# A hybrid decoder layer on one core: the order of the first loads, and the last stage's squares and products over two PSUM banks at once

## The reference, cut to what matters

```python
def _rmsnorm(x, g):
    xf = x.astype(jnp.float32)
    y = xf * lax.rsqrt(jnp.mean(xf * xf, axis=-1, keepdims=True) + EPS)
    return (y * g.astype(jnp.float32)).astype(x.dtype)

def _layer(x, mem_k, mem_v, s5_re, s5_im, lru_h, lru_conv, w):
    h = _rmsnorm(x, w["g_mix"])
    proj = h @ w["w_in"]                 # the first projection
    ...                                  # S5 and RG-LRU heads, output projection, cross attention
    x = x + _hier_moe(x, ...)            # two experts for each token, weighted
    ...
y_prompt = _rmsnorm(xp, g_final)
y_sample = _rmsnorm(xs, g_final)
```

## Time and profile before

| | before |
|---|---|
| three executions, us | 1136.73, 1139.09, 1140.87 |
| median, us | 1139.09 |
| the profiled execution, us | 1138.03 |
| its span, first to last instruction, us | 1136.2 |
| mean granted TensorE clock | 0.991 |
| PE busy | 1092.9 us, 96% |
| PE weight loads busy | 617.8 us, 54% |
| DVE busy | 625.3 us, 55% |
| ACT busy | 250.6 us, 22% |
| POOL busy | 80.9 us, 7% |

### The profile page before, as it was taken

One profiled execution on the slowest core, in us unless ns is written; L12 is line 12 of the kernel. 1 busy time (PEld: TensorE's weight loads), 2 busy tenths in 40 slices (PEclk: granted clock), 3 DMA queues, 4 the chain that ended last, 5 costly groups with the idle time before them and its releaser, 6 DMA issues.

```text
span 1136.2 us, 15240 instructions
## 1 busy us (share of the span) xinstructions
PE 1092.9 (96%) x6149; PEld 617.8 (54%) x6149; DVE 625.3 (55%) x1250; ACT 250.6 (22%) x531; POOL 80.9 (7%) x108
## 2 busy tenths in 40 slices
PE   6999999999999999999999999999899999999985
PEld 4666766677765444788866645554433333333322
DVE  4676499927857655843277776775632121121256
ACT  5200321356641111100033311111301011111115
POOL 5000010101000000000000000000111112121110
PEclk9999999999999999999999999999899999999998
DMA  9109350277471002300055451016779999999968
GB/s 296 46 1 221 30 42 1 74 203 274 151 275 23 0 1 88 135 1 1 9 200 200 148 217 43 20 56 228 282 270 402 417 415 418 415 417 416 366 251 315
DMA packets 65368, 209.27 MB, mean 184 GB/s; under 512 B 13560, under 2 KB 22416, under 8 KB 57072
## 3 DMA queue, kind: packets, MB, share of 16 engines
q1 hardware_dynamic: 54528, 177.68, 43.9%
q0 software_dynamic: 10640, 30.55, 7.6%
q10 hardware_dynamic: 128, 0.03, 0.0%
HBM read 187.05 MB, written 28.53 MB: 190 GB/s over the span
## 4 chain that ended last, share of the span: by engine, by line
PE 90%; DVE 5%; issue 2%; DMA 1%; ACT 1%; ACTq 0%; SPq 0%; DVEq 0%; POOLq 0%
PE bank L713 15%; PE bank L1230 15%; PE bank L876 9%; PE bank L941 8%; PE bank L1247 7%; PE bank L1071 6%; PE bank L685 5%; PE bank L835 3%; PE bank L973 2%; PE bank L1038 2%; PE bank L1218 2%; PE bank L802 2%; PE bank L1115 1%; PE bank L983 1%; PE bank L858 1%
## 5 line engine op out<-in xcount | busy, mean ns | idle before, releaser
L713 PE MATMUL bank<-arena 128*128 128x360 f32 (+1 forms) x576 | 177.7, 468 | 1.0 <-DVE arena L1633 0.9
L1230 PE MATMUL bank<-arena 128*32 128x512 f32 x1536 | 171.7, 599 | 1.0 <-DVE arena L2349 1.0
L713 PEld LDWEIGHTS bank<-arena 128*128 128x128 f32 x576 | 108.5, 190 | 64.8 <-issue 1.5
L1230 PEld LDWEIGHTS bank<-arena 128*32 128x32 f32 x1536 | 47.7, 110 | 106.6 <-issue 105.3
L1952 DVE TENSOR_TENSOR arena<-arena,bank 128x512 f32<-128x512 f32 (+3 forms) x56 | 68.3, 1220 | 66.6 <-PE bank L941 37.5
L876 PE MATMUL bank<-arena 128*128 128x272 f32 x448 | 103.0, 392 | 0.0
L1071 PE MATMUL bank<-arena 128*128 128x512 f32 x224 | 100.6, 598 | 0.5 <-DVE arena L2117 0.5
L941 PE MATMUL bank<-arena 128*128 128x512 f32 x224 | 97.7, 593 | 0.0
L876 PEld LDWEIGHTS bank<-arena 128*128 128x128 f32 x448 | 85.0, 190 | 17.4
L2353 DVE TENSOR_TENSOR arena<-arena,bank 128x256 f32<-128x256 f32 x24 | 10.1, 420 | 150.7 <-ACT arena L1539 150.7
L1247 PE MATMUL bank<-arena 128*32 128x512 f32 x768 | 86.8, 592 | 0.6 <-ACT arena L1542 0.6
(11 more groups left out here) (424 smaller groups left out, 1336.1 us busy)
## 6 DMA issues: line engine op xcount, KB each, us to landing
arena<-in_w_gate SPq DMA_DIRECT2D x32, 1024.0 KB, 9.4
arena<-in_w_up SPq DMA_DIRECT2D x32, 1024.0 KB, 15.4
arena<-in_w_down SPq DMA_DIRECT2D x32, 1024.0 KB, 16.4
arena<-in_ck SPq DMA_DIRECT2D x8, 1024.0 KB, 7.2
arena<-in_cv SPq DMA_DIRECT2D x8, 1024.0 KB, 5.3
arena<-work_moe SPq DMA_DIRECT2D x16, 512.0 KB, 7.4
arena<-in_w_in SPq DMA_DIRECT2D x3, 2048.0 KB, 14.9
arena<-in_x SPq DMA_DIRECT2D x8, 512.0 KB, 6.0
```

What stands on the lines that cost most here:

```text
L713: last = nc.tensor.matmul(b[:, 0:w], win[slot][:, k, m * P:m * P + P], ht[:, k, c0:c0 + w], start=k == 0, stop=k == KD - 1)
L1230: last = nc.tensor.matmul(bank[2 + j % 2][t0:t0 + QT, :].rearrange("p (h n) -> p h n", h=2), xgt[j % 2][:, k, t0:t0 + QT], gu[e % GUB][:, ...
```

## The change

There are five edits.

1. SP's order at the front: tiles 0 to 2, then the first third of `w_in`, then the convolution state and nine vectors (`VECS[3:]`), then the three tables; then a wait for the `w_in` transfer to land, and then tiles 3, 4 and 5. Six of those vectors were on ACT's queue before.
2. ACT issues three vectors (`VECS[:3]`) rather than nine ahead of its table load.
3. The eight PSUM banks are one tensor, so that one instruction can read two neighbouring banks. ACT's work for a PE tile is then one square of 1024 columns and one root, rather than two squares, an identity and a root; DVE's is one product of 1024 columns rather than two of 512.
4. PE no longer waits for `fin_x` ahead of the identity products; inside the branch for overflowing experts it waits for one more semaphore (`xya_ok`) instead.
5. DVE's order at the end: sums of 8 and 0; output of 8; sum of 2; output of 0; sum of 4; outputs of 1 and 2; sum of 6; outputs of 3 to 7.

```diff
-        bank = [ctx.enter_context(nc.psum_tensor(f"bank{b}", [P, 512], f32)) for b in range(8)]
+        psum = ctx.enter_context(nc.psum_tensor("banks", [P, 8 * 512], f32))
+        bank = [psum[:, 512 * b:512 * b + 512] for b in range(8)]
...
             for n in range(3):
                 load_x(n)
+            load_win(0, 0)
             sp.dma_start(cstin[0:NB * 3 * CT, :], I["state_lru_conv"]).then_inc(sem["par_in"], 16)
-            for name, rows in VECS[9:]:
+            for name, rows in VECS[3:]:
                 sp.dma_start(parin[COL[name]:COL[name] + rows, :], I[name]).then_inc(sem["par_in"], 16)
-            load_win(0, 0)
-            load_x(3)
             for src, dst in ((I["lam_re"], q16[0:GP, 2, :]), (I["lam_im"], q16[0:GP, 3, :]), (I["log_dt"], ptmp[0:GP, 256:258])):
                 sp.dma_start(dst, src).then_inc(sem["lam_in"], 16)
-            for n in range(4, 6):
+            sp.wait_ge(sem["win_in0"], 16)
+            for n in range(3, 6):
                 load_x(n)
             load_win(1, DH)
...
+                pe.wait_ge(sem["xya_ok"], XT)
                 pe.wait_ge(sem["xyd_ok"], XT + len(ZORDER))
...
-            pe.wait_ge(sem["fin_x"], 1)
             pe.wait_ge(sem["f_dg"], 2 * len(FPE))
...
-            for name, rows in VECS[:9]:
+            for name, rows in VECS[:3]:
                 act.dma_start(parin[COL[name]:COL[name] + rows, :], I[name]).then_inc(sem["par_in"], 16)
...
-                    link(nc.scalar.activation(squaresf[:, 0:512], bank[2 * j][:, :], ACT.Square, accum_out=ssq[:, i:i + 1]))
-                    link(nc.scalar.activation(squaresf[:, 512:1024], bank[2 * j + 1][:, :], ACT.Square, accum_out=srs[:, j:j + 1]))
-                    link(nc.scalar.activation(srs[:, j:j + 1], srs[:, j:j + 1], ACT.Identity, scale=1.0 / D, bias=zero1[:, 1:2]))
-                    nc.scalar.activation(rstd[:, i:i + 1], ssq[:, i:i + 1], ACT.Sqrt, scale=1.0 / D, bias=srs[:, j:j + 1]).then_inc(sem["f_std"], 1)
+                    link(nc.scalar.activation(squaresf[:, :], psum[:, 1024 * j:1024 * j + 1024], ACT.Square, accum_out=ssq[:, i:i + 1]))
+                    nc.scalar.activation(rstd[:, i:i + 1], ssq[:, i:i + 1], ACT.Sqrt, scale=1.0 / D, bias=zero1[:, 1:2]).then_inc(sem["f_std"], 1)
...
-                    for hf in range(2):
-                        cols = slice(hf * 512, hf * 512 + 512)
-                        last = V.scalar_tensor_tensor(xres[:, i, cols], bank[2 * j + hf][:, :], rstd[:, i:i + 1], gfin[:, cols], MUL, MUL)
-                    last.then_inc(sem["f_out"], 1)
+                    V.scalar_tensor_tensor(xres[:, i, :], psum[:, 1024 * j:1024 * j + 1024], rstd[:, i:i + 1], gfin[:, :], MUL, MUL).then_inc(sem["f_out"], 1)
...
-            for i in (8, 0, 2):
+            for i in (8, 0):
                 fsum(i)
-            for i in (8, 0):
-                fout(i)
+            fout(8)
+            fsum(2)
+            fout(0)
             fsum(4)
-            for i in (1, 2):
-                fout(i)
+            fout(1)
+            fout(2)
             fsum(6)
```

## The result

The changed kernel takes 1141.36 us (median of 22 executions, 1139.6 to 1143.76), the kernel before, beside it, 1139.34 (22 executions, 1136.73 to 1142.2). The ratio is 1.0023 with a 95% interval of 1.0016 to 1.0029: slower by 2.6 us (1.8 to 3.3), inside 0.3%, where 1141.3 had been forecast. The two medians by themselves are 2.0 us apart. Beside e9, e10 and e11 the kernel before had two slow executions of 23, of 1177.63 and 2935.26 us, which the ratios leave out.

A forecast was written before the change was run, and what follows sets the result against it. PE's chain of waits (90% of the span) was taken as the bound, with DVE's work setting the end. Plus 4.0 at the front and minus 1.8 at the end gave 1139.09 + 2.2 = 1141.3 us, 8-in-10 range 1136.0 to 1144.0.

The forecast's parts named there:

- The small loads behind the weights: Front: ten small loads land after the weights on SP's queue, shifting the projection to 21.0 us, plus 4.0 us.
- The 14.1: Front: time in us when tiles 0 to 2, 13 small loads and first weights are all through, bounds 13.0 to 15.0.
- the 12%: Front: data rate lost in a us with small packets, some 0.3 us over the few, used for the lower bound.
- ACT's shorter list: Front: six fewer issues start tile 0's transposes 1.2 us earlier, worth nothing while PE waits for the vectors until 14.1.
- Tiles 3 to 5: Front: loads issued after the first weights land still come before PE asks, cover over 4 us, so nothing.
- DVE's order and the long products: Last stage: reordered DVE work and one product in place of two, together minus 1.8 us, bounds minus 0.8 to 2.4.
- The products' term: Last stage: one 1024-column product takes 1.28 us instead of a pair's 1.41, four times 0.13 saved, taken as 0.5.
- the term for DVE's order: Last stage: tile 8's output fills the hole ahead of tile 2's sum, which starts at 1116.64; minus 1.29 us.
- The cover of 5 us: End: DVE reaches tile 7 5 us after PE's last product ended, so PE's earlier identity products gain zero.
- B: Rival, front: small loads pass the weights, ACT's earlier start gives minus 1.2, total 1136.1 us; chance 0.16.
- C: Rival, front: PE idles, its clock rises only inside the projection, up to 3.3 us more, 1144.6; chance 0.16.
- D: Rival, last stage: two-bank reads or loads hold DVE, gaining only 0.3 us, total 1142.8; chance 0.08.

The follow-up runs named there:

- e9: Kernel before plus changed end, wide PE products, ACT's three-vector list, six other vectors on SP ahead of the first weights; 1133.71 against 1140.52 us, ratio 0.9943.
- e10: Kernel before with only tiles 3, 4 and 5 moved behind the wait for the first weights; 1139.5 against 1140.52 us, ratio 0.9994.
- e11: Kernel before plus only five 512-column identity products on PE at the front; 1138.82 against 1140.52 us, ratio 0.9982.
- e1: Changed front with the last stage of the kernel before; 1143.42 against 1138.74 us, ratio 1.0042.
- e3: Kernel before with only state_lru_h (16 KB) moved behind the first weights on SP's queue; 1143.9 against 1138.74 us, ratio 1.0041.
- e12: Changed kernel with the first weights issued behind the ten small loads, no products added; 1136.24 us against the kernel before's 1139.49, ratio 0.9978.
- e2: Front of the kernel before with the changed last stage; 1138.41 against 1138.74 us, ratio 0.9992.
- e5: Front of the kernel before, changed last stage, plus five 512-column identity products on PE at the front; 1136.0 against 1139.63 us, ratio 0.9975.
- e6: Changed kernel plus 512-column identity products: three ahead of tile 0, four in the wait, one after; 1139.25 us against the kernel before's 1139.63, ratio 1.0005.
- e7: Front of the kernel before, changed last stage, but PE's wait for fin_x put back; one execution, 1138.43 us.
- e8: Front of the kernel before, changed last stage, but DVE's old order (sums of 8, 0, 2 first); one execution, 1138.85 us.
- e4: Changed kernel plus 24 identity products of 128 columns on PE between tile 0 and the vectors' wait; 1138.91 us against the kernel before's 1138.74, ratio 1.001.

## Why the prediction was right

**The small loads behind the weights (plus 4.0).** Right in mechanism and near in size: 21.44 - 17.04 = 4.40 in the changed kernel and 4.02 in e1. The vectors' transpose, forecast at 14.1 and at most 15.0, came at 14.59 and 14.46. e3 shows the mechanism by itself, and e12 that the rest of the changed front costs nothing that its time can tell. The Trainium skill's ring order ("DMA: Bandwidth & Descriptors", section "Queues, rings and completion order") agrees with e3's 13.80. What the Trainium skill says in the section "Issuing engines are not separate DMA queues" of the same page, that issuing from several engines only saves issue time, does not fit e3: ACT's last small load was issued there at 3.99, behind the weights' 3.42, and ACT's queue was through by 9 us, while `state_lru_h`, issued at 3.88 on SP's queue, came at about 13.75. The reasoning that the same bytes are through at the same time in any order was off in its parts: the weights landed 1.3 us earlier than before, not a few tenths, and the small loads 1.8 us behind them. The sum of the two errors is half a us. The 14.1 was not the time of that set alone either: the DMA engines had moved 4.48 MB by then in the kernel before, and 3.79 in e10, where tile 3 was not behind the weights, which landed at 13.8 all the same. And the 12% were put down to small packets, but from 7 to 8 us the rate before was 329 GB/s with 36 of them among 192. The 6.92 us from the vectors' transpose to the projection were 6.85 and 6.60.

**ACT's shorter list (nothing here).** Right. PE was ready 1.3 us earlier and waited; the 1.3 us turn up as soon as the vectors are there (e12).

**Tiles 3 to 5 (nothing).** Right, by e10, whose interval runs from 1.7 us faster to 0.3 slower.

**DVE's order and the long products (minus 1.8).** Right in direction and mis-sized: minus 0.94 in the changed kernel and minus 1.21 in e2 by the trace; minus 0.9 us by time in e2, with an interval from minus 1.9 to plus 0.1. The products' term held: 1.28 us each, 0.13 saved. What was mis-sized is the term for DVE's order, in the start of tile 2's sum. It was put right behind tile 8's output, 1116.64 - 1112.45 = 4.2 us behind the first sum, with the load taken to come 4.1 us behind it, as in the one trace at hand; it came at 4.8 in both kernels, and DVE waited 0.5 us and took up 0.6 later than forecast. In the changed kernel another 0.2 us were lost to tile 1's root: PE, freed from its wait for `fin_x`, had finished its identity products early and then stood 4.34 us, and its next products ran at the lower level of the clock. (In e2 PE stood 4.40 us, the granted clock read 0.64 from 1114 to 1118 us, and nothing was lost at tile 1.) PE's timeline, and the stretch from 1122 to 1128 us, against the earlier trace rows:

```profile
1111.19 7.11 PE L1302 MATMUL banks<-arena,ident 128*128 128x512 f32 x16 [0.92 <-ACT arena L1546]
1122.64 10.05 PE L1306 MATMUL banks<-arena 128*128 128x512 f32 x16 [4.34 <-DMA arena<-work_moe]
```

```profile
1122.00:1128.00 6.00, 5.36 (x7) 2.24 (x8) 5.27 (x7) 2.75 (x7) 0.00 (x0) 0.50 1.01 388
```

DVE came to tile 1's output at 1127.71, and the root was ready at 1127.90. The cover of 5 us that the prediction names at tile 7 was there; at tile 1 it was not, and the prediction had looked only at the end of the chain. With both waits gone (e5, e6) the stage took 19.1 us, minus 1.65.

**The rivals.** B (small loads not late) fell with the first row of PE's timeline. C (the clock rises late, inside the projection) took place in the profiled execution: 7.46 us and not 5.18, plus 2.3. But it does not need the change. It took place in the profiled executions of e7, e8 and e10 as well, with the front of the kernel before, and it did not in e1, with the changed one. Whether the change makes it more frequent is open: without added products it is there in three of six traces with the small loads ahead of the weights and in two of three with one or ten behind. It makes the two profiled executions 5.8 us apart where the medians are 2.0. As a rival it was well priced and wrongly attached: it belonged on both sides. D (the last stage gives 0.3) fell by the traces, though half of its reason, a late load, was there.

**The sum.** By the trace, 4.4 - 0.9 = 3.5 us from the change itself, with the clock's 2.3 set aside; by time, 2.6 (1.8 to 3.3). By e1 and e2, 4.8 - 0.9 = 3.9, with intervals of 1.5 and 1.0 us on them. The trace's 3.5 is a little above the interval by time, and what part of that us is the clock's place in other executions is open. That the median came within 0.1 us of 1141.3 is luck: by the traces the front cost 0.4 us more than forecast and the end gave 0.9 less, which would have made 3.5 and not 2.2.

## What to carry to other kernels

In these runs a small load was as late as the 2 MB in front of it on its queue: issue what is small and waited for first, and count one small load behind a large one as the whole delay, since a shared semaphore waits for the last. Issuing the large one early bought nothing that was needed: issued at 2.17 it landed at 12.8, at 3.94 at 14.1, at 5.98 at 14.0 (e9, where the DMA rate fell to 101 GB/s from 7 to 8 us), and the projection began after 15.7 in all of them. And before a difference between two single profiles is put down to an edit, compare the same instructions' durations in several executions: here 2.3 us of clock looked like part of the change.

## What the runs showed of the hardware that had not been expected

- The granted clock reads 1.00 through the front of most traces while eight 128-column transposes take 1.94 us there and 1.04 to 1.09 at full speed. In the changed kernel it reads 1.00 from 22 to 24 us too, while a 128x368 matmul takes 854 ns in the mean as against 472 at full speed; in e4, whose clock had risen and fell again, it reads 0.50 beside matmuls as slow. As far as these traces show, the column tells of changes, and the level before the first of them has to be read from durations.
- Three or four products of 512 columns ahead of tile 0 (e5, e6, e9, e11) took its eight transposes from 1.94 us to between 1.09 and 1.28 in each of the four traces; in e11 the projection's first matmuls were slow all the same.
- Ten small loads, 88 KB in all, landed 1.8 us after the 2 MB ahead of them, though the DMA engines moved only 23 GB/s in the us from 12 to 13 and 33 in the next. One load of 16 KB landed under 0.2 us after them (e3).
